# A decoder trunk in split single precision: three more groups of weights multiplied ahead of a head pair's first scores, with two small steps moved between engines

## What is computed

```
def hybrid_layer(x, ...):
    h = rms_norm(x, norm_g)
    z = h @ w_in          # split into x_rnn, g_rnn, sc_b, sc_c, x_sc, g_sc, c_q, c_kv, k_rope, g_att, gates
    y_rnn = (rg_lru(x_rnn, ...) * silu(g_rnn)) @ rg_out
    y_sc = (sc_b * causal_depthwise_conv(sc_c * x_sc, sc_conv_w) * silu(g_sc)) @ sc_out
    y_att = (mla(c_q, c_kv, k_rope, ...) * silu(g_att)) @ mla_out
    ...
def mla(...):             # 8 heads; q and k are normalised per head, rotary on the last 64 of 192
    q = rms_norm((rms_norm(c_q) @ w_uq), qn_g); k = rms_norm(concat(ckv @ w_uk, k_r), kn_g)
    o = softmax(q k^T / sqrt(192), causal) @ v
```

## Time and profile before

| | us |
|---|---|
| median of 3 runs (1774.89 to 1777.08) | 1775.55 |
| the profiled execution's own time | 1778.09 |
| its span, first to last instruction | 1776.3 |
| PE busy | 1723.0 (97%) |
| POOL busy | 1202.3 (68%) |
| DVE busy | 880.8 (50%) |
| ACT busy | 480.1 (27%) |

### The profile page before, as it was taken

One profiled execution on the slowest core, in us unless ns is written; L12 is line 12 of the kernel. 1 busy time (PEld: TensorE's weight loads), 2 busy tenths in 40 slices (PEclk: granted clock), 3 DMA queues, 4 the chain that ended last, 5 costly groups with the idle time before them and its releaser, 6 DMA issues.

```text
span 1776.3 us, 32266 instructions
## 1 busy us (share of the span) xinstructions
PE 1723.0 (97%) x11956; PEld 1611.7 (91%) x11956; DVE 880.8 (50%) x1289; ACT 480.1 (27%) x859; POOL 1202.3 (68%) x1365
## 2 busy tenths in 40 slices
PE   7999999999999999999999999999999999999999
PEld 7989898989999999999999797988898888888887
DVE  6955647574454451222358556475745554522221
ACT  4423233242233331101134232332322233311110
POOL 7764747375787777777756647474757888877773
PEclk9999999999999999999999999999999999999999
DMA  4321212222322223222432212122223222332233
GB/s 155 133 94 55 77 64 89 70 71 65 106 90 83 84 81 144 94 89 89 163 106 84 83 66 77 64 89 70 71 65 113 83 94 90 125 106 94 95 119 108
DMA packets 49407, 164.21 MB, mean 92 GB/s; under 512 B 6048, under 2 KB 7456, under 8 KB 49056
## 3 DMA queue, kind: packets, MB, share of 16 engines
q1 hardware_dynamic: 41328, 146.56, 24.5%
q10 hardware_dynamic: 8032, 17.03, 2.9%
HBM read 152.21 MB, written 10.81 MB: 92 GB/s over the span
## 4 chain that ended last, share of the span: by engine, by line
PE 86%; DVE 9%; issue 4%; ACT 1%; DMA 1%; DVEq 0%; ACTq 0%
PE slots L507 76%; PE slots L572 4%; PE slots L605 2%; DVE early L1262 2%; PE slots L660 2%; PE slots L590 1%; DVE qr_hi_and_lo L1092 1%; DVE early L1280 1%; DVE kr_lo L1092 1%; DVE kn_lo L1092 1%; DVE qn_lo L1268 1%; DVE early L1287 1%; DMA residual_or_merged<-xt 1%; DVE spare L1288 1%; ACT early L897 0%
## 5 line engine op out<-in xcount | busy, mean ns | idle before, releaser
L419 POOL TENSOR_TENSOR w_lo<-w_raw,w_hi 128x256 fp32r<-128x256 f32 x1004 | 842.7, 869 | 20.9
L414 POOL TENSOR_SCALAR w_hi<-w_raw 128x1024 fp32r<-128x1024 f32 x251 | 288.2, 1148 | 400.0 <-PE slots L507 391.7
L507 PE MATMUL slots<-h_hi,w_hi 128*128 128x264 f32 (+1 forms) x2112 | 530.3, 315 | 14.9 <-ACT sc_c L971 13.0
L507 PE MATMUL slots<-h_lo,w_hi 128*128 128x264 f32 (+1 forms) x2112 | 521.3, 311 | 0.0
L507 PE MATMUL slots<-h_hi,w_lo 128*128 128x264 f32 (+1 forms) x2112 | 520.4, 311 | 0.0
L507 PEld LDWEIGHTS slots<-h_hi,w_hi 128*128 128x128 f32 x2112 | 348.2, 191 | 36.8 <-issue 15.7
L507 PEld LDWEIGHTS slots<-h_hi,w_lo 128*128 128x128 f32 x2112 | 346.1, 191 | 20.1
L507 PEld LDWEIGHTS slots<-h_lo,w_hi 128*128 128x128 f32 x2112 | 346.8, 191 | 18.5
L507 PE MATMUL slots<-branch_hi,w_hi 128*128 128x264 f32 (+1 forms) x576 | 144.5, 314 | 11.6 <-DVE branch_lo L1104 9.6
L507 PE MATMUL slots<-branch_lo,w_hi 128*128 128x264 f32 (+1 forms) x576 | 143.1, 312 | 0.0
L507 PE MATMUL slots<-branch_hi,w_lo 128*128 128x264 f32 (+1 forms) x576 | 142.9, 312 | 0.0
(11 more groups left out here) (234 smaller groups left out, 2824.9 us busy)
## 6 DMA issues: line engine op xcount, KB each, us to landing
w_raw<-w_units SPq DMA_DIRECT2D x251, 512.0 KB, 3.3
stream<-sc_acc ACTq DMA_DIRECT2D x16, 264.0 KB, 3.0
sc_back<-stream SPq DMA_DIRECT2D x2, 2112.0 KB, 8.0
x_old<-stream SPq DMA_DIRECT2D x16, 264.0 KB, 4.2
stream<-residual_or_merged ACTq DMA_DIRECT2D x16, 264.0 KB, 2.5
ab_raw<-w_units SPq DMA_DIRECT2D x8, 512.0 KB, 4.0
residual_or_merged<-xt ACTq DMA_DIRECT2D x4, 528.0 KB, 8.6
stream<-xt ACTq DMA_DIRECT2D x1, 2112.0 KB, 11.2
```

The source lines that it names most:

```text
L414: pool.tensor_scalar(hi, raw, 1.0, 1.0, ALU.mult, ALU.mult).then_inc(sem("hi_part"), 1)
L419: op = pool.tensor_tensor(lo[:, cols], raw[:, cols], hi[:, cols].bitcast(F32), ALU.subtract)
L507: mm = pe.matmul(out[:, a_, 0:t1 - t0], w(k), x(k)[:, t0:t1], start=(n == 0), stop=(n == 3 * ks - 1))
```

## The change

The first `FILLS[1]` grows from 9 to 16 k-tiles, so that 5 + 3 + 16 = 24, all of `c0`, `x0` and `g0`, stand ahead of the first scores in place of 17; the five steps of the first head then get 4, 4, 4, 5 and 5 k-tiles in place of 5, 5, 6, 6 and 7. The sum over a pair stays 80. `qr` and the filling units swap slots 0 and 1. The scaling of `qr` goes from DVE to ACT, as an activation of kind Identity right behind the Square that reads the same slot. ACT's `sc_copy(0)` moves from behind the statistics to between the copies `kn_hi` and `kr_hi`. In the steps of the first head, `sc_tanh(0)` (ACT) moves from step 1 to step 0, `sc_out(0)` from 3 to 2 and the last `sc_conv` piece from 2 to 3 (DVE).

```diff
--- before.py
+++ after.py
@@ -71,7 +71,7 @@
 
 
 FILL = ("c0", "x0", "g0", "b0", "ga0", "c1", "x1", "g1", "b1", "ga1")
-FILLS = (5, 9, 5, 5, 6, 6, 7, 2, 6, 6, 7, 7, 6)
+FILLS = (5, 16, 4, 4, 4, 5, 5, 2, 6, 6, 7, 7, 6)
 STAGES = {"NORM": (1, 0, 0), "CQ": (1, 6, 2), "ATT": (4, 12, 0), "RG": (4, 8, 0), "MR": (4, 4, 0),
           "MS": (4, 4, 0), "OUT": (2, 4, 0)}
 
@@ -84,10 +84,10 @@
            ("sum_kr", 2, "cq_mm"), ("stat_q", 1, "cq_mm")],
     "ATT": [("va", 2, "att_mm"), ("kn0", 0, "att_mm"), ("kn1", 1, "att_mm"), ("vb", 3, "unit_used"),
             ("sum_k0", 0, "att_mm"), ("sum_k1", 1, "att_mm"), ("qn0", 2, "att_mm"), ("qn1", 3, "unit_used"),
-            ("qr", 0, "att_mm"), ("stat_q", 3, "att_mm"),
-            ("c0", 1, "unit_used"), ("x0", 0, "unit_used"), ("g0", 1, "unit_used"), ("b0", 0, "unit_used"),
-            ("ga0", 1, "unit_used"), ("c1", 0, "unit_used"), ("av0", 1, "att_mm"), ("x1", 0, "unit_used"),
-            ("g1", 1, "unit_used"), ("b1", 0, "unit_used"), ("ga1", 1, "unit_used"), ("av1", 0, "att_mm")],
+            ("qr", 1, "att_mm"), ("stat_q", 3, "att_mm"),
+            ("c0", 0, "unit_used"), ("x0", 1, "unit_used"), ("g0", 0, "unit_used"), ("b0", 1, "unit_used"),
+            ("ga0", 0, "unit_used"), ("c1", 1, "unit_used"), ("av0", 0, "att_mm"), ("x1", 1, "unit_used"),
+            ("g1", 0, "unit_used"), ("b1", 1, "unit_used"), ("ga1", 0, "unit_used"), ("av1", 1, "att_mm")],
     "RG": [("x0", 0, "unit_used"), ("x1", 1, "unit_used"), ("g0", 2, "unit_used"), ("g1", 3, "unit_used"),
            ("a0", 0, "rg_mm"), ("a1", 1, "rg_mm"), ("i0", 2, "rg_mm"), ("i1", 3, "rg_mm"),
            ("mg0", 0, "unit_used"), ("mg1", 1, "unit_used"), ("my0", 2, "unit_used"), ("my1", 3, "unit_used")],
@@ -906,12 +906,21 @@
                     act.wait_ge(*ready("ATT", l, p, "qr"))
                     act.activation(halves(ct[6][:]), slot(slot_of("ATT", "qr")), ACT.Square).then_inc(
                         sem("q_squared"), 1)
+                    act.activation(halves(ct[7][:]), slot(slot_of("ATT", "qr")), ACT.Identity, bias=zero,
+                                   scale=hparam(l, QR_G)).then_inc(freed("ATT", "qr"), 1)
 
                     act.wait_ge(*was_read("ATT", l, p, "qr"))
                     turn_halves(spare[0][:], ct[7][:], "qr_turned")
                     for h in range(2):
                         act.wait_ge(*at("k_full", l, p, h + 1))
                         act.activation(kn_hi[:, h, :], ct[2 + h][:], ACT.Copy).then_inc(sem("k_hi"), 1)
+                    def sc_copy(s):
+
+                        act.wait_ge(*ready("ATT", l, p, f"c{s}"))
+                        act.activation(halves(s_c[:]), slot(slot_of("ATT", f"c{s}")), ACT.Copy).then_inc(
+                            freed("ATT", f"c{s}"), 1)
+
+                    sc_copy(0)
                     for h in range(2):
                         act.wait_ge(*at("kr_scaled", l, p, h + 1))
                         act.activation(kr_hi[:, h, :], ct[4 + h][:], ACT.Copy).then_inc(sem("krp_hi"), 1)
@@ -965,12 +974,6 @@
                         act.wait_ge(*was_read("ATT", l, p, f"av{h}"))
                         act.activation(tile(y_hi, 2 * p + h), probs_out[h], ACT.Copy).then_inc(sem("att_hi"), 1)
 
-                    def sc_copy(s):
-
-                        act.wait_ge(*ready("ATT", l, p, f"c{s}"))
-                        act.activation(halves(s_c[:]), slot(slot_of("ATT", f"c{s}")), ACT.Copy).then_inc(
-                            freed("ATT", f"c{s}"), 1)
-
                     def sc_tanh(s):
 
                         act.wait_ge(*ready("ATT", l, p, f"g{s}"))
@@ -987,7 +990,6 @@
                                       s_acc[:]).then_inc(sem("sc_stored"), 16)
 
                     probs_out = [spare[0][:], spare[1][:]]
-                    sc_copy(0)
                     for n in range(10):
                         soften(n)
                         if n == 4:
@@ -997,7 +999,7 @@
                         if n == 8:
                             sc_tanh(1)
                         turned_part(n)
-                        if n == 1:
+                        if n == 0:
                             sc_tanh(0)
                         if n == 4:
                             sc_store(0)
@@ -1269,9 +1271,6 @@
                                                  hparam(l, QN_G), halves(qn_hi[:, g, :]).bitcast(F32), ALU.mult,
                                                  ALU.subtract).then_inc(freed("ATT", f"qn{g}"), 1)
 
-                    dve.wait_ge(*at("q_squared", l, p, 3))
-                    dve.tensor_scalar(halves(ct[7][:]), slot(slot_of("ATT", "qr")), hparam(l, QR_G), None,
-                                      ALU.mult).then_inc(freed("ATT", "qr"), 1)
 
                     dve.wait_ge(*at("kr_done", l, 0, 1))
                     for h in range(2):
@@ -1429,9 +1428,9 @@
                         if n == 1:
                             sc_gate(0)
                         if n == 2:
+                            sc_out(0)
+                        if n == 3:
                             sc_conv(0, 2)
-                        if n == 3:
-                            sc_out(0)
                             sc_product(0)
                         if n == 4:
                             gate(0)
```

## The result

| | before | changed |
|---|---|---|
| median of the runs on one chip, us | 1775.22 (1773.64 to 1777.08) | 1723.12 (1722.76 to 1723.46) |
| the profiled execution's own time, us | 1778.09 | 1722.76 |
| its span, us | 1776.3 | 1721.0 |
| mean granted clock | 0.982 | 0.996 |

What follows compares the result with a forecast made beforehand. PE, busy 97%, was taken as the bound, with only its idle time and clock to win: 37.1 + 19.5 - 1.6 = 55.0 us off 1778.1 gives 1723.1; 2.5 us less for the median, 1720.5 us, range 1716.5 to 1732.

Steps and rivals of the forecast that it cites:

- standstill ahead of the first scores: PE's two waits per pair, for `c0`'s copy and the last query operand, would go: 4.64 us a pair, 37.1 us.
- clock in the first steps: First step of each pair, slowed by a low clock after the standstill, would run at full clock: 19.5 us won.
- new waits in the steps of head 0: Head 0's steps, with 7 fewer k-tiles of cover, would cost 0.2 us a pair, 1.6 us (bounds 0 and 14).
- rival (1): DVE and POOL get in each other's way in head 0, costing 4 to 14 us: 1723 to 1734; chance 0.12.
- the slack had been put at 0.25: Head 0, step 0: scaled rows would be ready before PE wants them, by 0.5 us, in layer 1 0.25.
- The slack was put at 1.1 us: Ahead of the first scores: operands at 292.6, PE free to start at 292.8, wanting them at 293.9; 0.9 in layer 1.
- the sentence on what ACT takes over: Scaling of `qr` leaves DVE's queue, everything behind 0.7 us sooner; ACT's Identity costs 0.79 us where it waited anyway.
- The rule of the Trainium skill that was weighed: In head 0, a two-SBUF-input VectorE instruction would wait for a whole GpSimd one, pricing their interference in the upper half.
- (2): Part of the wait for operands ahead of the first scores stays, 1 us a pair, 8 us: 1728; chance 0.07.
- (4): Slower: head 0's five short steps don't cover the softmax, PE waits each turn at 1.2 GHz: 1879; chance 0.03.
- (5): Nothing changes, PE waiting as long for some missed slot or unit: 1775.5; chance 0.02.
- (3): Clock still falls in the first steps, for a cause other than the standstill; only 35.5 us won: 1740; chance 0.06.

Runs made afterwards that it cites:

- experiment 3: The changed kernel with ACT's copy of `c0` back behind the statistics and the table load; 1724.94 us, ratio 0.9722.
- experiment 6: The changed kernel with 6 k-tiles ahead of the query statistics in place of 5, and 15 after them in place of 16; 1714.31 us, ratio 0.9666.
- Experiment 4: The changed kernel with the scaling of `qr` back on DVE; 1716.92 us, ratio 0.9685.
- experiment 9: The changed kernel itself, unedited, measured again; 1725.39 us, ratio 0.9715.
- experiment 1: The kernel before with only the new table of fills (24 k-tiles ahead of the first scores); 1745.77 us, ratio 0.9844.
- experiment 8: The kernel before with the new table of fills and the new step order, nothing else; 1733.84 us, ratio 0.9764.
- experiment 5: The changed kernel with the first head's convolution steps (`sc_tanh`, `sc_out`, last `sc_conv`) in the old order; 1735.95 us, ratio 0.9800.
- experiment 2: The changed kernel with the old table of fills (17 k-tiles ahead of the first scores); 1763.64 us, ratio 0.9933.
- experiment 7: The changed kernel with the twenty one-column statistics matmuls in a row, their three k-tiles behind them; 1725.99 us, ratio 0.9732.
- experiment 10: The changed kernel with the scaling of `qr` on DVE and 6 k-tiles ahead of the statistics; 1717.65 us, ratio 0.9670.

## Why the prediction was right, point by point

The forecast was 1720.5 us in a range of 1716.5 to 1732; the run gave 1723.1, and 52 us gained where 55.0 had been summed up. The terms of the sum, against the two profiled executions, good to some tenths of a microsecond each:

| term | predicted | measured |
|---|---|---|
| standstill ahead of the first scores | 37.1 | 37.1: both waits are gone in all eight pairs |
| clock in the first steps | 19.5 | 19.9 |
| new waits in the steps of head 0 | -1.6 | -1.3 |
| the statistics' wait for POOL | 0 | -4.3 |
| clock behind the statistics | 0 | -3.4, in one pair |
| elsewhere, the remainder | 0 | 7.3 |

*Clock.* A first step with four k-tiles takes 3.54 us in layer 0 and 3.38 in layer 1, from its first score to that of the next step; with a fifth (0.735 and 0.705 us) the eight steps make 33.4 us of work out of the 53.3 of the earlier trace rows.

*Steps of head 0.* The four-k-tile steps hold. DVE and POOL do meet there, as rival (1) says, but the price is small: PE's weight loads wait 3.0 us in all for L1347. By the starts of the scores, the second and third steps are each 0.1 us longer in layer 1 than the same steps where they don't wait (3.72 against 3.59 us, 4.06 against 3.95, the latter in pairs of experiments 3 and 6), where the slack had been put at 0.25; in layer 0 it is less than 0.1 us for the whole head.

*Operands.* The slack was put at 1.1 us; 1.5 are seen, of which 0.5 is PE's own lateness. DVE's queue does gain 0.6 of the 0.7 us by the move (16.7 us in place of 17.3 from `qn_lo` to the end of the last operand). Experiment 4, which has no wait for the operands, shows that it was not needed.

**The step that failed** is the sentence on what ACT takes over: taking the scaling off DVE was counted as 0.7 us won, and POOL was looked at only for its weights ("POOL: it has split `b0`..."). What it does between them, the two adds on which PE's statistics wait, was missing. There was no slack at all in that place: before, PE lost 0.19 us there (178.03 to 178.47), now 0.72. That is 0.53 us a pair, 4.3 in all, and the clock falls behind that wait now and then.

The rule of the Trainium skill that was weighed (SBUF — State Buffer, Who interferes with whom) named the right two engines, and I applied it to the wrong place. The Trainium skill says there of a DVE instruction with two SBUF inputs that it contends with a GpSimd instruction that reads SBUF, and of DVE's two-port modes that whoever issues first holds the ports for the whole instruction. The trace agrees with the second wording for these products too: the product that starts 0.02 us ahead holds the add up by 0.5 us, and the add then holds the next product up until its end (1.71 us in place of 0.70).

By experiment 4 the move of the scaling cost 4 us by the ratios and 6 by the medians, rather than winning anything. The intervals of the two ratios overlap; that of the changed kernel's second measurement (0.9702 to 0.9729, experiment 9) lies clear above experiment 4's (0.9672 to 0.9698). The wait and the fall are worth 7.7 us, and the longer first steps of experiment 4 take 2.8 of it back.

*Elsewhere.* 3.4 us are falls of the clock at the start of the kernel and of layer 1, which the profile of before has (from 21 and 946 us) and that of the changed kernel has not or shorter; 1.1 are waits at the start of the kernel that differ between executions. Another 2.2 are no scatter. The two waits for L1372 are in all three profiles with the old slots (before, experiments 1 and 8) and in none of the nine with the swapped ones: the attention result of the last head now leaves slot 1, and the next stage starts in slot 0. The forecast had the swap at nothing. 0.6 us is left.

The run shown of before was 2.5 us above its median and the changed kernel's at its own, which is why 55.3 us between profiles are 52.1 between medians. The two missing terms are 7.7 us, and the forecast missed by 2.6: that it came so near is in part luck. The 2.2 us of the swap, which it did not have either, and the scatter of the profiles hide two thirds of the error.

*The rivals.* (2), (4) and (5) didn't come, and neither did (3) where it was put: the clock is whole in the first steps, as forecast, but it falls in another place, behind the statistics. The order of the steps was worth more than I said, 12 to 17 us (experiments 5 and 8), through a slot and not through the softmax.

Where the 52 us come from, by the ratios times 1775 us, each step with the pieces before it in place: the table of fills 28 us (0.9844), the order of the steps 14 (0.9764), the swapped slots and the early copy 14 (0.9685), and the scaling on ACT takes 4 back (0.9706; 5 by the 0.9715 of experiment 9). Each of these is uncertain by 3 to 4 us. The third agrees with what it removes, 14 us from start to start for the wait for `c0` and 2 for that of the swap; the swap and the early copy were not run apart. Everything but the table wins 12 us by itself (experiment 2) and 24 on top of the table: its pieces are worth that much only once the first scores no longer hold PE up.

## What to carry to other kernels

When fill work is moved ahead of a wait, follow every slot and every other engine's queue to its new due time, the side jobs of a slow engine too: each of three late pieces here (a copy, a tanh, an add) held the pair up by itself. An instruction that seems free to move off a busy engine may be what keeps that engine out of another one's way; look at what its neighbours will now run beside, and which of the two starts first. A standstill of PE can cost the slow clock behind it besides its own length, so that removing the last of it may be worth more than its idle time: the last 4 us of waiting were worth 4 to 9 (experiments 4 and 6).

## What the runs showed of the hardware that I had not expected

- After 1.6 to 1.8 us of standstill ahead of `g0` the clock stayed at 2.4 GHz in all eight pairs (experiment 1). At one of 3.4 us it fell to 1.2 GHz in seven of seven (experiment 2), and came back in the midst of unbroken matmuls, 6 us later in the pair shown.
- A wait of 0.56 us ahead of the statistics' twenty matmuls of one column (with two k-tiles between them, in experiment 7 with none) was followed by a fall in one or two pairs of eight in each of the six profiled executions that have it (the changed kernel, experiments 2, 3, 5, 7 and 9), nine of 46 pairs, and not in the same ones each time. The same twenty matmuls without the wait were followed by none in 50 pairs (before, experiments 1, 4, 6, 8 and 10, and one pair each of 3 and 5). So these small matmuls alone don't do it; whether the wait would without them is not shown, and experiment 7, made for that question, decided nothing. A longer wait of the same kind, 0.84 us ahead of one-column matmuls at the start of each layer, was followed by a fall in 12 of 12 profiles in layer 0 and in 8 of 12 in layer 1. The Trainium skill (TensorE: Matmul & The Clock Gate, HAM oscillation) tells of a clock that falls again in each idle gap between bursts of matmuls, and in the section behind it (A second HAM failure mode: psum-queue depth-cycling) of short idle times between groups of matmuls that are enough if they are frequent. Experiment 2 agrees with the first. The falls behind the statistics are nearer to the second, though the idle time here comes once a pair.
- A product of 528 columns on DVE with two SBUF operands took 0.70 us when it started ahead of one of POOL's adds, and the add then 1.86 in place of 1.34. The same kind of product, started during the add, took 1.24 us in the kernel before and 1.71 in the changed one, and ended 0.56 to 0.58 us after the add in all 96 pairs.
